# One change to a two-block transformer kernel in split float32: mq, Ag and Aq by halves of the tokens, Newton steps with one instruction fewer, and the last quarter of wo2a's products partly moved

## What is computed

```python
def _layer(x, mem, ...):                     # block 1, two layers
    h = x @ w_in                             # q/kv ranks, sb, fox, mem_q, gates, merge rank
    q  = _rms_norm(c_q,  q_norm)  @ w_qb     # "mla": two norms over features
    kv = _rms_norm(c_kv, kv_norm) @ w_kvb
    y_mla, y_sb, y_fox                       # three causal attentions
    mk, mv = jnp.split(mem @ w_mem_kv, 2, axis=-1)
    y_mem = _memory_attention(mem_q, mk, mv)
    for n in range(4):
        merged += merge_g[:, :, n] * ((branches[n] * silu(gate_z[:, :, n])) @ w_branch[n])
    return _layer_norm(ALPHA * x + merged @ w_out, ln_g, ln_b)

def second_block(x, ...):                    # block 2, two layers
    for l in range(2):
        h = _rmsnorm(x, norm_g[l])
        z = h @ w_in[l]
        q_a, k_a = axial_rope(_rmsnorm(q_a)), axial_rope(_rmsnorm(k_a))   # per head of 64
        o_a, o_b, o_c, o_d                   # dense, window, neighbourhood, differential
        mix = concat([o_a * silu(g_a), o_b * silu(g_b), o_c * silu(g_c), o_d * silu(g_d)])
        x = x + mix @ w_out[l]
    return _rmsnorm(x, final_g)
```

## Time and profile before

| | before |
|---|---|
| median of 3 runs | 1554.25 us (1554.24 to 1555.29) |
| profiled execution | 1553.3 us |
| its span | 1551.2 us |
| mean granted clock of TensorE | 0.974 of full speed |
| TensorE busy | 1418.2 us, 91% |
| VectorE busy | 903.9 us, 58% |
| ScalarE busy | 682.7 us, 44% |
| GpSimd busy | 367.7 us, 24% |

### The profile page before, as it was taken

One profiled execution on the slowest core, in us unless ns is written; L12 is line 12 of the kernel. 1 busy time (PEld: TensorE's weight loads), 2 busy tenths in 40 slices (PEclk: granted clock), 3 DMA queues, 4 the chain that ended last, 5 costly groups with the idle time before them and its releaser, 6 DMA issues.

```text
span 1551.2 us, 21240 instructions
## 1 busy us (share of the span) xinstructions
PE 1418.2 (91%) x8026; PEld 1092.2 (70%) x8026; DVE 903.9 (58%) x1705; ACT 682.7 (44%) x1478; POOL 367.7 (24%) x265
## 2 busy tenths in 40 slices
PE   6799998999989999999998799997999799998997
PEld 5666685777987576767788666665777656665776
DVE  3646437557672553484576575568655466558655
ACT  2445444455233553445552444335443444335443
POOL 1224122245231321222451111410001112310011
PEclk9999999999999999999999799998999899998999
DMA  6542211225343121211263323511313322511211
GB/s 213 139 103 68 76 61 41 62 61 204 109 138 80 29 82 56 82 40 51 67 224 90 88 55 69 116 55 49 95 62 96 82 65 58 116 55 48 96 62 55
DMA packets 191448, 131.72 MB, mean 85 GB/s; under 512 B 91764, under 2 KB 181492, under 8 KB 191348
## 3 DMA queue, kind: packets, MB, share of 16 engines
q1 hardware_dynamic: 179302, 110.19, 26.0%
q10 hardware_dynamic: 12046, 20.19, 3.9%
HBM read 118.03 MB, written 12.32 MB: 84 GB/s over the span
## 4 chain that ended last, share of the span: by engine, by line
PE 69%; DVE 18%; ACT 8%; issue 3%; DMA 1%; ACTq 1%; POOL 0%; DVEq 0%; SPq 0%; POOLq 0%
PE pb L1390 18%; PE pb L1391 16%; PE pb L1392 16%; PE pb L1468 6%; PE pb L1412 5%; PE pb L1446 4%; ACT prob L1524 2%; ACT wh L1542 2%; ACT tmp L1524 1%; DVE wl L1851 1%; DVE small L2116 1%; DVE xl L1858 1%; PE pb L1430 1%; DVE scr L2138 1%; DMA wr<-w_in 1%
## 5 line engine op out<-in xcount | busy, mean ns | idle before, releaser
L2283 POOL TENSOR_TENSOR wl<-wr,wh 128x512 fp32r<-128x512 f32 x170 | 237.2, 1395 | 896.8 <-ACT wh L1542 893.0
L1390 PE MATMUL pb<-xh,wl 128*128 128x512 f32 (+1 forms) x832 | 352.2, 423 | 29.2 <-DVE xl L1858 21.7
L1391 PE MATMUL pb<-xl,wh 128*128 128x512 f32 (+1 forms) x832 | 322.6, 388 | 0.0
L1392 PE MATMUL pb<-xh,wh 128*128 128x512 f32 (+1 forms) x832 | 322.0, 387 | 0.0
L1851 DVE TENSOR_TENSOR wl<-wr,wh 128x512 fp32r<-128x512 f32 x200 | 164.0, 821 | 164.6 <-ACT wh L1542 164.3
L1390 PEld LDWEIGHTS pb<-xh,wl 128*128 128x128 f32 x832 | 162.4, 195 | 110.0 <-issue 60.1
L1542 ACT CAST wh<-wr 128x512 fp32r<-128x512 f32 x370 | 211.0, 603 | 58.8 <-PE pb L1392 31.2
L1392 PEld LDWEIGHTS pb<-xh,wh 128*128 128x128 f32 x832 | 162.4, 195 | 31.9
L1391 PEld LDWEIGHTS pb<-xl,wh 128*128 128x128 f32 x832 | 163.3, 196 | 24.2 <-issue 3.8
L1524 ACT ACTIVATE prob<-prob,small 128x512 f32<-128x512 f32 (+3 forms) x128 | 76.2, 597 | 147.2 <-DVE small L2093 147.1
L1446 PE MATMUL pb<-cst,prob 128*128 128x128 f32 x768 | 118.9, 276 | 23.9 <-ACT prob L1524 13.1
(11 more groups left out here) (196 smaller groups left out, 2448.6 us busy)
## 6 DMA issues: line engine op xcount, KB each, us to landing
wr<-w_in SPq DMA_DIRECT2D x40, 1024.0 KB, 5.4
wr<-w_in SPq DMA_DIRECT2D x48, 256.0 KB, 4.5
wr<-w_out SPq DMA_DIRECT2D x10, 1024.0 KB, 6.1
wr<-w_branch SPq DMA_DIRECT2D x48, 128.0 KB, 2.3
x<-prob SPq DMA_DIRECT2D x12, 512.0 KB, 2.6
wr<-w_out SPq DMA_DIRECT2D x48, 128.0 KB, 3.0
wr<-w_mem_kv SPq DMA_DIRECT2D x4, 1024.0 KB, 8.0
prob<-x ACTq DMA_DIRECT2D x2, 2048.0 KB, 10.3
```

The costliest lines, as they stand in the source:

```text
L1390: e.matmul(ps, ll, rh, start=start, stop=False)
L1391: e.matmul(ps, lh, rl, start=False, stop=False)
L1392: t = e.matmul(ps, lh, rh, start=False, stop=stop)
L2283: t = e.tensor_tensor(wl[:, j % 2, c0:c1], wr[:, j % 2, c0:c1], wh[:, j % 2, c0:c1].bitcast(F32), ALU.subtract)
```

## The change

Five things change.

1. `mq` of block 1's layer 1 is opened by halves: both column pieces of `mkv1` run without a break, `mq` runs over tokens 0 to 255, then tile 3's features, then tokens 256 to 511. The last norm of the layer before (tile 3's) is put behind `mkv1`.
2. In both layers of block 2, `Ag` and `Aq` are both opened by halves: Ag first half, Aq first half, features 2 and 3, Ag second half, gate, Aq second half. The two banks of `Aq` are held from the beginning. While this goes on no casts are ticked, so those of `Akv` stand behind the gate's two tanh on ScalarE.
3. The buffer for the squares in branch A comes from ring `TA` instead of `TM`.
4. `newton_wide` takes three instructions instead of four, `newton` three instead of four, and `newton`'s first no longer waits for the root, but only for the sum of squares (or the variance).
5. Piece m = 3 of `wo2a` runs tiles 0 and 1 beside branch C; tiles 2 and 3 (36 matmuls of 256 columns, two `acc`) run after the `wo2b` parts of tiles 0 and 1. Casts of the next piece are held until then.

```diff
+    def halves(w, ep, half, held):
+
+        for c in range(2):
+            drain(gemm("fm", w, 128 * c, 128 * c + 128, ("x", ep), range(8), n=256, b=held[c], off=256 * half,
+                       end=half == 1))
+
     def opened(w, ep, between):
 
         held = [GR[0].take() for _ in range(2)]
-        for half in range(2):
-            for c in range(2):
-                drain(gemm("fm", w, 128 * c, 128 * c + 128, ("x", ep), range(8), n=256, b=held[c], off=256 * half,
-                           end=half == 1))
-            if not half:
-                between()
+        halves(w, ep, 0, held)
+        between()
+        halves(w, ep, 1, held)
         return held
 
...
 
-    def gate(name, ep, br, l, between=None):
-        w = wnext(name)
-        held, u = opened(w, ep, between) if between else [], None
+    def gate(name, ep, br, l, w=None, held=()):
+        u = None
...
         run(features(0, i, (X[i],)))
 
-    def last_features(ep, *src):
-        for i in (2, 3):
+    def last_features(ep, src=(), tiles=(2, 3)):
+        for i in tiles:
             run(features(ep, i, src and (src[i],)))
         give(*src)
...
         w = wnext("mq")
-        if l:
-            held = [drain(gemm("fm", w, 128 * c, 128 * c + 128, ("x", l), range(8))) for c in range(2)]
-        else:
-            held = opened(w, l, lambda: last_features(l, *X))
+        held = opened(w, l, lambda: last_features(l, X, (3,) if l else (2, 3)))
...
             parts = mem_parts(1)
-            for turned in ((0, 1), (2,), (3,), ()):
+            for turned in ((0, 1), (2,), ()):
                 next(parts)
                 advance_late(late)
                 for i in turned:
                     run(features(1, i, (X[i],)))
             rest_of(parts)
-            give(*X)
+            while advance_late(late):
+                pass
 
...
         ep = 2 + l
-        for x in gate(br + "g", ep, br, l, (lambda: last_features(ep)) if br == "A" else None):
+        two, held = [None, None], [(), ()]
+        if br == "A":
+            two, held = [wnext(br + "g"), wnext(br + "q")], [[GR[0].take() for _ in range(2)] for _ in range(2)]
+            st["hold"] = True
+            for w, h in zip(two, held):
+                halves(w, ep, 0, h)
+            last_features(ep)
+            halves(two[0], ep, 1, held[0])
+        for x in gate(br + "g", ep, br, l, two[0], held[0]):
             if x is not None:
                 box["u"] = x
             yield
+        if br == "A":
+            st["hold"] = False
+            halves(two[1], ep, 1, held[1])
         if br == "C":
             w = "Cq"
...
         put("tabs", l=l, br=br)
-        w = wnext(br + "q")
+        w = two[1] if br == "A" else wnext(br + "q")
         sides = []
 
         def beside(g):
...
                 wdone(w)
                 w = wnext(br + "kv")
             c0 = 128 * (n % 2)
-            b = yield from beside(gemm("fm", w, c0, c0 + 128, ("x", ep), range(8)))
+            if br == "A" and n < 2:
+                b = held[1][n]
+            else:
+                b = yield from beside(gemm("fm", w, c0, c0 + 128, ("x", ep), range(8)))
             tm = TM.take()
-            sq = TM.take() if br == "A" else None
+            sq = TA.take() if br == "A" else None
             put("pair", l=l, br=br, n=n, b=b, tm=tm, sq=sq)
             give(b)
             sides.append(behind(n, tm, sq))
...
                 for i in range(2):
                     held[i] = yield from gemm("tok", w, 0, 256, ("y2", l), range(4), tile=i, end=False, stop=False)
                 rest_of(before)
-            for i in range(4):
+            for i in range(2 if m == 3 else 4):
                 b = yield from gemm("tok", w, 0, 256, ("y2", l), range(4 if i in held else 0, 6), tile=i, b=held.get(i),
                                     start=i not in held)
                 put("acc", l=l, m=m, i=i, b=b)
                 give(b)
                 yield
-            wdone(w)
+            if m < 3:
+                wdone(w)
+        box["w"] = w
+
+    def out_left(l, w, i):
+
+        b = drain(gemm("tok", w, 0, 256, ("y2", l), range(6), tile=i))
+        put("acc", l=l, m=3, i=i, b=b)
+        give(b)
 
     for l in range(2):
         box, tail = {}, iter(())
...
             u = box["u"]
             box = {}
-            fill = project(l, "ABDC"[n + 1], box) if br != "C" else out_partial(l, tail)
+            fill = project(l, "ABDC"[n + 1], box) if br != "C" else out_partial(l, tail, box)
...
             tail = then(tail)
         finish_main(tail)
         first["w"] = wnext("wo2b")
+        st["hold"] = True
         X0, X = [ER.take() for _ in range(4)], [TT.take() for _ in range(4)]
...
             yield
 
         for i in range(4):
+            if i == 2:
+                for n in (2, 3):
+                    out_left(l, box["w"], n)
+                    advance_late(late)
+                wdone(box["w"])
+                st["hold"] = False
             for m in range(2):
                 b = part(i, m, 0)
                 part(i, m, 1, b)
...
                 t = act(prob[:, 0, 0:1024], xres[:, i, :], ACT.Square, accum_out=st[:, 30:31])
-                t.then_inc(a_fn.sem, a_fn.mark(ends=s["x0"]))
+                t.then_inc(a_fn.sem, a_fn.mark(("rmssum", ep, i), ends=s["x0"]))
                 w.wait_ge(a_fn, a_fn.n)
                 act(st[:, 32:33], st[:, 30:31], ACT.Ln, 1.0 / D, C("eps6")).then_inc(a_fn.sem, a_fn.mark())
...
             x = nwt[:, :]
             for g, n in tn.free():
                 w.wait_ge(g, n)
-            e.tensor_tensor(x, o, o, ALU.mult).then_inc(v_fn.sem, v_fn.mark())
+            e.scalar_tensor_tensor(x, v, dim * 1e-6, o, ALU.add, ALU.mult).then_inc(v_fn.sem, v_fn.mark())
             w.wait_ge(v_fn, v_fn.n)
-            e.scalar_tensor_tensor(x, v, dim * 1e-6, x, ALU.add, ALU.mult).then_inc(v_fn.sem, v_fn.mark())
+            e.scalar_tensor_tensor(x, x, -0.5 / dim, o, ALU.mult, ALU.mult).then_inc(v_fn.sem, v_fn.mark())
             w.wait_ge(v_fn, v_fn.n)
-            e.tensor_scalar(x, x, -0.5 / dim, 1.5, ALU.mult, ALU.add).then_inc(v_fn.sem, v_fn.mark())
+            e.scalar_tensor_tensor(o, x, 1.5, o, ALU.add, ALU.mult).then_inc(v_fn.sem, v_fn.mark(*key, ends=(tn,)))
             w.wait_ge(v_fn, v_fn.n)
-            e.tensor_tensor(o, o, x, ALU.mult).then_inc(v_fn.sem, v_fn.mark(*key, ends=(tn,)))
-            w.wait_ge(v_fn, v_fn.n)
-
-        def newton(rs, var, scale, eps, x, y):
-            e.tensor_scalar(y, var, scale, eps, ALU.mult, ALU.add).then_inc(v_fn.sem, v_fn.mark())
+
+        def newton(rs, var, scale, eps, x, y, root):
+
+            e.tensor_scalar(y, var, -0.5 * scale, -0.5 * eps, ALU.mult, ALU.add).then_inc(v_fn.sem, v_fn.mark())
+            w.wait_ge(a_fn, a_fn.at(root))
             w.wait_ge(v_fn, v_fn.n)
             e.scalar_tensor_tensor(x, rs, y, rs, ALU.mult, ALU.mult).then_inc(v_fn.sem, v_fn.mark())
             w.wait_ge(v_fn, v_fn.n)
-            e.tensor_scalar(x, x, -0.5, 1.5, ALU.mult, ALU.add).then_inc(v_fn.sem, v_fn.mark())
-            w.wait_ge(v_fn, v_fn.n)
-            e.tensor_tensor(rs, rs, x, ALU.mult).then_inc(v_fn.sem, v_fn.mark())
+            e.scalar_tensor_tensor(rs, x, 1.5, rs, ALU.add, ALU.mult).then_inc(v_fn.sem, v_fn.mark())
             w.wait_ge(v_fn, v_fn.n)
 
         def parts_of(period):
...
                     t.then_inc(v_fn.sem, v_fn.mark())
                 else:
-                    w.wait_ge(a_fn, a_fn.at(("lnroot", l, i)))
-                    newton(st[:, 26:27], st[:, 25:26], 1.0, 1e-5, st[:, 27:28], st[:, 28:29])
+                    newton(st[:, 26:27], st[:, 25:26], 1.0, 1e-5, st[:, 27:28], st[:, 28:29], ("lnroot", l, i))
                     t = e.scalar_tensor_tensor(x, x, st[:, 26:27], lnp[:, 1, :], ALU.mult, ALU.add)
                     t.then_inc(v_fn.sem, v_fn.mark(("normed_x", l, i)))
             elif k == "rms2":
                 ep, i, st = s["ep"], s["i"], stats[:, s["i"], :]
-                w.wait_ge(a_fn, a_fn.at(("rmsroot", ep, i)))
-                newton(st[:, 32:33], st[:, 30:31], 1.0 / D, 1e-6, st[:, 33:34], st[:, 34:35])
+                w.wait_ge(a_fn, a_fn.at(("rmssum", ep, i)))
+                newton(st[:, 32:33], st[:, 30:31], 1.0 / D, 1e-6, st[:, 33:34], st[:, 34:35], ("rmsroot", ep, i))
                 w.wait_ge(d_res, d_res.at(("ln", 1) if ep == 2 else ("grow", ep - 3)))
                 dst = xres[:, i, :] if ep == 4 else setB[:, D * i:D * i + D]
```

More of the change, by code:

```diff
@@ L401, in features @@
             yield
[L403 to L405 removed]
+    def gate(name, ep, br, l, w=None, held=()):
+        u = None
+        w = wnext(name) if w is None else w
         for c in range(2):
@@ L979, in project, with out_partial @@
         yield
-    def out_partial(l, before):
+    def out_partial(l, before, box):
         for m in range(4):
```

## The result

The kernel became slower: 1557.18 us (median of 20 runs) against 1554.7 us for the kernel before (20 runs); the ratio is 1.0023, with an interval of 1.0013 to 1.0032. The forecast was 1547.7 us in a range of 1541.0 to 1553.0. The profiled execution has a span of 1555.8 us, 4.6 more than before.

The account below looks back on a forecast made before the run. The prediction took TensorE, busy 1418.2 of 1551.2 us, as the bound. Its terms 2.8 + 0.5 - 1.0 + 0.3 + 3.0 + 0.9 = 6.5 us, off 1554.25, gave 1547.7 us, range 1541.0 to 1553.0.

Parts of the forecast that it names:

- the wait before the third turn: Branch A, block 2: TensorE waits once for VectorE's scaling of n = 2, 3.1 us, plus 1.0 for a held instruction.
- The term of block 2's layer 0: Branch A of block 2's layer 0, opened by halves: gain 0.5 us, bounds -1.0 and 3.5.
- second rival: TensorE's clock falls behind the new waits of 4.1 us: 1.5 us more in each layer, 1550.7 us; chance 0.15.
- The term of layer 0 to layer 1: Block 2, from layer 0 into layer 1's opening: a loss, -1.0 us, bounds -3.0 and 2.0.
- mq by halves: Block 1's layer 1: mq ends earlier when opened by halves, gain 2.8 us, bounds 2.0 and 3.6.
- The Newton steps: Shorter wide steps gain 3.0 us in block 1's two layers and 0.9 us in branch D.
- the assumption that the new step is not held beside GpSimd: Wide Newton step in block 1's mla: first instruction, reading PSUM, is not held; first step 2.2 us instead of 3.75.
- Its term of 1.5 in block 1's layer 0: Shorter wide Newton steps save 0.46 + 1.04 = 1.5 us in each layer of block 1.
- The end of the program: Sums of tile 3 no longer behind a norm, less wo2b's stall: gain 0.3 us, bounds -0.5 and 1.3.
- The stall at wo2b's beginning: First wo2b matmuls wait for late weight chunks: 0.7 to 1.7 us per layer, taken as 1.0.
- The rival of the thinner cover in branch C: 27 matmuls fewer beside branch C's last rounds lose 3.3 us a layer: 1554.3 us, no change; chance 0.16.
- The fourth rival: Branch A: GpSimd's subtractions hold six VectorE chain instructions a layer, 11 us in all: 1558.7 us, slower; chance 0.07.

Follow-up runs that it names:

- the run with the wait of 3.73: Short Newton steps and mq by halves together in the kernel before, block 2's openings and outputs untouched: 1545.08 us, ratio 0.9941.
- both orders tried with the groups together: Changed kernel with the rotation tables' load put early, 1548.63 us; the same with the scaling of n = 2 ahead of two Newton steps, 1550.16 us.

## Why the prediction was wrong, step by step

**The step that failed** is the sentence of the prediction on the wait before the third turn, "In their place comes one wait ... The wait is 3.1", which let VectorE's chain begin "from the end of the first turn". It counted what stands ahead of the chain on VectorE and TensorE, and not what the chain reads. The rotation tables come by a DMA that the edit put behind one more weight piece (four more DMAs) on SyncE's queue. The prediction looked at the order of three engines and not at that queue. Instead of 3.1 plus 1.0 the waits were 7.13 and 7.65. With the tables early they were 3.47 each: the arithmetic of the chain itself was right.

**The term of block 2's layer 0** was a gain of 0.5, of which 0.6 lay ahead of Ag; for the stretch from Ag on the forecast was 0.1 more, and 5.4 more were measured (70.4 for 65.1). Of this the tables are 3.8 (66.6 with them early). A further 1.6 is the clock behind the wait, which the prediction had as its second rival, with a chance of 0.15: it happened in both layers, also behind the 3.47. The term also booked to the halves of Aq what another edit does: by the Newton steps alone the wait of 4.16 ahead of Ag's second half went to 3.2, the 48 matmuls behind it ran at full clock, and the stretch was 63.4 (64.9 in the run with the wait of 3.73). Against that kernel the halves cost 7.0 in layer 0. Ag's second half began 19.0 us after the first, as forecast (19.1).

**The term of layer 0 to layer 1**, -1.0, became -8.5 by the stretches of the two profiles: 1.2 gained up to Ag, as forecast (2.2 less 1.0), and 9.8 lost behind it, where the forecast comes to 2.2 (5.86 more ahead of Ag's second half, 3.1 less behind it, 0.5 of wait less). The tables are 4.4 of the 9.8 (63.1 for 58.7 with them early, to the attention's first product, 53.3 before), the clock behind the third turn 1.7 with the tables early, and the clock behind the wait of 1.88 another 1.5. That last drop the prediction didn't have: it took 1.00 behind 1.88 from one row. The edit isn't shown to cause it, since it also came with Aq whole, in one of two profiles. Ag began 17.1 us ahead of its second half, for 17.7 forecast.

**What held.** mq by halves was forecast at 2.8 and measured 2.2 by the ratio, 3.0 by the medians. The Newton steps were forecast at 3.0 + 0.9 and the small ones with 0.6 more: 4.5, measured 6.4 by the ratio and 4.4 by the medians. The wide step in the mla projections went from 3.75 to 2.57 (108.60 to 111.17), not to 2.2: the assumption that the new step is not held beside GpSimd was half wrong. Its term of 1.5 in block 1's layer 0 held even so. From TensorE's wait for ScalarE at 76 to 79 us to its wait in the mla projections it took 48.1 to 48.6 us in the five profiles with the old steps, 45.5 to 47.0 in the nine with the new. The saving of 0.46 a step rests on the removed instruction's 0.43; in branch A that one had taken 0.65 to 0.74.

```profile
108.60 0.68 DVE L1844 SCALAR_TENSOR_TENSOR scr<-pb,tmp 128x512 f32<-128x512 f32 x1
109.31 1.09 DVE L1846 SCALAR_TENSOR_TENSOR scr<-scr,tmp 128x512 f32<-128x512 f32 x1
110.44 0.69 DVE L1848 SCALAR_TENSOR_TENSOR tmp<-scr,tmp 128x512 f32<-128x512 f32 x1
```

The instruction with its input in PSUM took 0.68 and the next one, with two inputs in SBUF, was held instead, 1.09. In branch A of the run with the Newton steps alone it was held in all six steps, 1.48 to 1.73, so there the step was no shorter than before. The end of the program was forecast at 0.3 and gained 0.3 with the Newton steps; they alone gained 0.5, so the quarter costs 0.2. The stall at wo2b's beginning is 0.69, at the lower bound. The rival of the thinner cover in branch C did not show: no wait of TensorE stands there between 1126 and 1180. The fourth rival, slower by VectorE behind GpSimd, was right in its sign and place and wrong in its mechanism: one instruction of the chain was held in each layer, as counted.

**The sum, with measured terms.** Newton steps and mq, 9.2 gained; the quarter, little. Aq by halves is all that lies between the kernel with Aq whole (0.9918 and 0.9923) and the changed one (1.0023): it costs 15.5 to 16.3 us. Of these the early tables give back 8 (1.0023 to 0.9974 is 7.6, 8.5 by the medians). The other 7 to 9 I put down to the half of Aq that now stands ahead of Ag's second half, the 3.47 us, and the clock behind them; they were not tried one by one. That the wait alone lowers the clock was argued from the rows in which both stand together (0.78, 0.76 and 0.67 behind 3.47, 3.47 and 7.65; 1.00 behind 0.65), not tried by itself. And the wait's length does not decide it alone: behind 1.88 ahead of Ag's second half it was 1.00 in thirteen places of the fourteen profiles and about 0.71 in six others.

The Trainium skill has the fall of the clock behind idle time as a rule, in "TensorE: Matmul & The Clock Gate", Part 1: the array that idles falls to half of its 2.4 GHz. The rows agree behind 5.24 (0.61 in the changed kernel, from 851.72) and behind 3.47; behind 3.17, ahead of Ag's second half in the run with Aq whole, the clock held at 1.00:

```profile
851.72:858.50 6.78, 6.78 (x37) 6.78 (x38) 4.62 (x12) 3.00 (x7) 0.00 (x0) 0.61 0.20 79
```

```profile
864.80:870.70 5.90, 5.90 (x49) 5.90 (x50) 0.69 (x1) 0.69 (x1) 0.00 (x0) 1.00 1.02 218
```

The columns are those of the windows above, the first of the changed kernel, the second of the run with Aq whole.

## What to carry to other kernels

When work is moved forward on one engine, follow each operand of the moved instructions back to its DMA, and see what stands ahead of that DMA on the queue now; a small load behind a big one that waits for a buffer is as late as that buffer. When an edit removes one wait, compare with the kernel that has all the other edits, not with the one before all of them: a cheaper edit may already have taken the same wait. And moving a piece within a chain that is longer than the work beside it can only move the wait, as it did here; the plain order, one group after the other between the matmuls, was better than both orders tried with the groups together.

## What the runs showed of the hardware

The same program's clock of TensorE drops at different places in different executions, and each drop costs 1.5 to 1.9 us: the stretch of some 62 us that ends at the merge of block 1's layer 1 took 63.4 us in two profiles (one is that of before) and 61.5 to 61.9 in the twelve others. The difference lies behind one wait of 2.4 us, where the clock was 0.83 in the two and 1.00 in the changed kernel. Behind the waits of 3.47 to 8.57 us (104 in the fourteen profiles from 70 us on) the clock of the next 6 us was 0.77 or less; behind those of 1.88 and of about 3 us it was low in some and 1.00 in others. The beginning varies as well: TensorE's wait for ScalarE at 76 to 79 us ended up to 2.6 us apart, without an edit ahead of it. An edit of 2 us can't be seen in one profile's span, only in its own stretch or in several rounds. On VectorE, beside a GpSimd subtraction, an instruction with two inputs in SBUF took 1.1 to 1.8 us instead of 0.69, at 109.31 here and at 891.23 above. One input in SBUF was enough in some rows (1.40 us for 0.43 at 56.88 in the profile of before). Of some sixty with an input in PSUM that stood beside such a subtraction in the changed kernel's profile, none took over 0.75. So which instruction of a chain reads PSUM, and which one stands beside GpSimd, decided what the fusion saved.
